# Strassen's block products in half of the contraction of a down projection's unit pairs, one pipeline for all pairs, and the mixer's tables loaded in the mixer

## What is computed

```python
def swiglu(h, w1, w3, w2):
    return (jax.nn.silu(h @ w1) * (h @ w3)) @ w2

h = rmsnorm(x, g_ffn1[l])
x = x + 0.5 * swiglu(h, w1_a[l], w3_a[l], w2_a[l])
h = rmsnorm(x, g_mix[l])
...                       # in-projection, two attentions, gates, out-projection
h = rmsnorm(x, g_ffn2[l])
x = x + 0.5 * swiglu(h, w1_b[l], w3_b[l], w2_b[l])
return rmsnorm(x, g_final)
```

## Time and profile before

| | |
|---|---|
| time, median of 3 runs | 1125.85 us (1125.63 to 1126.07) |
| the profiled execution's own time | 1127.22 us |
| its span | 1125.3 us |
| mean granted TensorE clock | 0.997 of full speed |
| PE busy, matmuls | 1101.4 us (98%), 6033 |
| DVE busy | 770.2 us (68%), 1090 |
| ACT busy | 543.7 us (48%), 870 |
| share of the 16 DMA engines, main queue | 28.9% |

### The profile page before, as it was taken

How to read it: one execution, slowest core, us unless ns; L and a number is a source line. 1 busy time by engine, 2 the same in 40 slices (tenths; PEclk the granted TensorE clock), 3 DMA queues, 4 the chain that set the end, 5 groups by cost and what they waited for, 6 DMA issues and landing times.

```text
span 1125.3 us, 15594 instructions
## 1 busy us (share of the span) xinstructions
PE 1101.4 (98%) x6033; PEld 943.5 (84%) x6033; DVE 770.2 (68%) x1090; ACT 543.7 (48%) x870; POOL 2.7 (0%) x6
## 2 busy tenths in 40 slices
PE   8999999999999999999999999999999999999996
PEld 6888899988998788877777778788898899889985
DVE  7876378745868778678765556667774578637864
ACT  6554155523644456567755543425552355415642
POOL 0000000000000000000000000000000000000000
PEclk9999999999999999999999999999999999999999
DMA  8323233332324212111112113422233323333222
GB/s 295 96 75 113 75 113 113 113 94 94 93 73 131 79 39 75 56 38 53 51 57 75 52 57 96 142 94 94 90 104 106 95 94 113 94 94 113 82 68 75
DMA packets 34295, 103.18 MB, mean 92 GB/s; under 512 B 4144, under 2 KB 7472, under 8 KB 34224
## 3 DMA queue, kind: packets, MB, share of 16 engines
q1 hardware_dynamic: 34224, 102.21, 28.9%
HBM read 100.10 MB, written 2.10 MB: 91 GB/s over the span
## 4 chain that ended last, share of the span: by engine, by line
PE 85%; DVE 6%; ACT 4%; issue 3%; SPq 1%; DMA 1%; POOL 0%; POOLq 0%; DVEq 0%; ACTq 0%
PE acc_pair L1208 24%; PE acc_pair L1209 24%; PE acc_pair L1210 24%; PE pair_bank L1208 2%; PE pair_bank L1210 2%; PE pair_bank L1209 2%; DVE w_lo L785 1%; PE bank L1208 1%; PE bank L1210 1%; PE bank L1209 1%; ACT rope L646 1%; ACT w_hi L487 1%; DMA w_raw<-in_w13a 1%; PE bank L1216 1%; PE bank L1218 1%
## 5 line engine op out<-in xcount | busy, mean ns | idle before, releaser
L1208 PE MATMUL acc_pair<-xg_hi,w_hi 128*128 128x512 f32 (+1 forms) x693 | 265.5, 383 | 1.5 <-DVE w_lo L1016 1.5
L1209 PE MATMUL acc_pair<-xg_lo,w_hi 128*128 128x512 f32 (+1 forms) x693 | 259.8, 375 | 0.0
L1210 PE MATMUL acc_pair<-xg_hi,w_lo 128*128 128x512 f32 (+1 forms) x693 | 259.1, 374 | 0.0
L487 ACT ACTIVATE w_hi<-w_raw 128x1024 fp32r<-128x1024 f32 (+3 forms) x159 | 154.3, 976 | 147.9 <-PE acc_pair L1210 147.3
L785 DVE TENSOR_TENSOR w_lo<-w_raw,w_hi 128x1024 fp32r<-128x1024 f32 (+3 forms) x159 | 178.6, 1126 | 42.3 <-ACT w_hi L487 41.3
L1210 PEld LDWEIGHTS acc_pair<-xg_hi,w_lo 128*128 128x128 f32 x693 | 130.5, 188 | 24.6
L1208 PEld LDWEIGHTS acc_pair<-xg_hi,w_hi 128*128 128x128 f32 x693 | 130.8, 189 | 23.1 <-issue 2.8
L1209 PEld LDWEIGHTS acc_pair<-xg_lo,w_hi 128*128 128x128 f32 x693 | 131.0, 189 | 19.9 <-issue 0.7
L1210 PE MATMUL acc_pair<-hid_hi,w_lo 128*128 128x512 f32 x352 | 138.8, 394 | 0.0
L1209 PE MATMUL acc_pair<-hid_lo,w_hi 128*128 128x512 f32 x352 | 138.2, 393 | 0.0
L1208 PE MATMUL acc_pair<-hid_hi,w_hi 128*128 128x512 f32 x352 | 136.9, 389 | 0.0
(11 more groups left out here) (220 smaller groups left out, 2059.7 us busy)
## 6 DMA issues: line engine op xcount, KB each, us to landing
w_raw<-in_w13b SPq DMA_DIRECT2D x44, 512.0 KB, 3.6
w_raw<-in_w13a SPq DMA_DIRECT2D x40, 512.0 KB, 3.8
w_raw<-in_wmix SPq DMA_DIRECT2D x22, 512.0 KB, 3.5
w_raw<-in_w2a SPq DMA_DIRECT2D x16, 512.0 KB, 3.6
w_raw<-in_w2b SPq DMA_DIRECT2D x16, 512.0 KB, 3.5
w_raw<-in_wgate SPq DMA_DIRECT2D x8, 512.0 KB, 3.5
w_raw<-in_wend SPq DMA_DIRECT2D x8, 512.0 KB, 3.5
w_raw<-in_wo SPq DMA_DIRECT2D x8, 512.0 KB, 3.5
```

The costliest lines, as they stand in the source:

```text
L487: act.activation(w_hi[:, s, 0:width], w_raw[:, s, 0:width], ACT.Copy).then_inc(whi_done, 1)
L1208: pe.matmul(o, w_h, r_h, start=first, stop=False, skip_group_check=check)
L1209: pe.matmul(o, w_h, r_l, start=False, stop=False, skip_group_check=check)
L1210: return pe.matmul(o, w_l, r_h, start=False, stop=last, skip_group_check=check)
```

## The change

The down units are run in pairs as well: of the 8 tiles (6 in the last chunk) of contraction, 4 are multiplied as 7 block products of 2 tiles and 256 columns (`HQ = 2`), the others as before. This is done for all down pairs but the last of each FFN, so for 11 pairs in each. The hidden tiles' sums are made by DVE while the gate and up pairs run: whenever the second tile of a block pair of `hid_pairs` has been multiplied, `hidden_sums` makes four sums of 256 columns (into the two `sq` buffers, as `hsum`), ACT splits off `th_hi`, DVE `th_lo`. The order of the down weights' tiles follows (`hid_order`). Gate, up and down pairs go through one `fast_pair` on each engine, in which the work on the pair before (`take_pair` or `take_outputs`) comes at fixed places. `cos`, `sin`, `mask_dl`, `rope2` and `roped` move to the mixer's room; the three loads are issued in the mixer and DVE's multiplication of the tables stands ahead of its part in the first scores.

```diff
+HQ = 2
+HID_PAIRS = {(0, 0): ((0, 1), (4, 5)), (1, 0): ((2, 3), (4, 5))}
...
+def hid_pairs(b, c):
+    return HID_PAIRS.get((b, c), ((0, 1), (2, 3)))
...
+def hid_order(b, c):
+    pairs = hid_pairs(b, c)
+    front = [p[0] for p in pairs] + [p[1] for p in pairs]
+    return front + [k for k in range(CHUNKS[c][1]) if k not in front]
...
+def fast_pairs(b):
+    base = (FFN_A, FFN_B)[b]
+    units = []
+    for c, (f0, n) in enumerate(CHUNKS):
+        at = chunk_base(base, c)
+        units += [at + 2 * j for j in range(n) if f0 + j >= PLAIN[b]]
+        units += [at + 2 * n + m for m in range(0, KD - (2 if c == len(CHUNKS) - 1 else 0), 2)]
+    return units
...
+def hidden_pair(u):
+    b, c, j = gate_tile(u)
+    for q, p in enumerate(hid_pairs(b, c)):
+        if p[1] == j:
+            return HQ * (len(CHUNKS) * b + c) + q
+    return None
...
...
                 load(u, 0, A["wmix"][u - MIX])
+                if u == MIX + 5:
+                    sp.wait_ge(unit_done, MIX)
+                    sp.dma_start(cos[:], A["cos"]).then_inc(late_loaded, 16)
+                    sp.dma_start(sin[:], A["sin"]).then_inc(late_loaded, 16)
+                    sp.dma_start(mask_dl[:].bitcast(mybir.dt.uint16), A["mask_dl"]).then_inc(late_loaded, 16)
...
+            def hidden_sums_hi(u):
+                h = hidden_pair(u)
+                if h is not None:
+                    act.wait_ge(hsum_done, 4 * (h + 1))
+                    act.activation(th_hi[:, :, h % HQ, :], hsum, ACT.Copy).then_inc(th_hi_done, 1)
...
+            def squares(u, n_next):
+                _, _, m = down_unit(u)
+                for k in (0, 1):
+                    act.wait_ge(acc_read[(u + k) % RING], reads(u + k, 0) + 1)
+                    square(m + k, n_next)
+            def fast_pair(u, prev, nxt, n_next):
                 g = fast_index(u)
                 r1, r3, r4, r2 = quarters(u)
+                before = gate_tile(prev) if prev is not None else None
+                turn = before is not None and down_unit(u) is not None
+                f = hidden_tile(prev)
                 split_hi(u + 2, 0, unit_width(u + 2))
                 act.wait_ge(p6_done, g + 1)
                 act.activation(r3, r2, ACT.Copy, scale=-1.0).then_inc(seed2, 1)
@@ -574,43 +668,43 @@
                     act.wait_ge(p5_added, g)
                 act.activation(p5[:, 0], bank_p5, ACT.Copy, scale=-1.0).then_inc(p5_copied, 1)
                 act.activation(p5[:, 1], bank_p5, ACT.Copy).then_inc(p5_copied, 1)
+                if turn:
+                    silu(prev, f)
                 act.wait_ge(p7_done, g + 1)
                 act.activation(r4, r2, ACT.Copy).then_inc(seed3, 1)
-                if not first:
-                    silu(u - 2, f - 1)
-                if last:
+                if turn:
+                    hidden_hi(f, before[2])
+                elif before is not None:
+                    silu(prev, f)
+                if prev is not None and before is None and down_unit(prev)[1] == len(CHUNKS) - 1:
+                    if down_unit(prev)[2] == 0:
+                        act.preload_act_table_set("sqrt_and_others")
+                    squares(prev, n_next)
+                if nxt is None:
                     split_hi(u + 3, 0, unit_width(u + 3))
                 else:
                     split_second_hi(u + 3)
-                if not first:
-                    hidden_hi(f - 1, slot - 1)
-                if last:
-                    silu(u, f)
-                    hidden_hi(f, slot)
-                else:
-                    seed_first(u + 2)
...
+            def ffn(b, n_norm, n_next):
+                plain_pairs((FFN_A, FFN_B)[b], NF * b, n_norm)
+                pairs = fast_pairs(b)
+                for u, prev, nxt in zip(pairs, [None] + pairs, pairs[1:] + [None]):
+                    fast_pair(u, prev, nxt, n_next)
+                u = pairs[-1] + 2
+                for k in (0, 1):
+                    if u + k + 2 < UNITS:
+                        split_hi(u + k + 2, 0, unit_width(u + k + 2))
+                    if k == 0:
+                        squares(u - 2, n_next)
+                    act.wait_ge(acc_read[(u + k) % RING], reads(u + k, 0) + 1)
+                    square(KD - 2 + k, n_next)
...
+            def add_fifth(u):
+                g = fast_index(u)
+                dve.wait_ge(unit_done, u + 2)
+                dve.wait_ge(p5_copied, 2 * (g + 1))
+                late = acc_pair[u % RING // 2][:].rearrange("p (n c) -> p n c", n=2)[:, :, HALF:SEQ]
+                dve.tensor_tensor(late, late, p5, ALU.add).then_inc(p5_added, 1)
+                dve.wait_ge(p5_added, g + 1)
...
+            def hidden_sums(u):
+                h = hidden_pair(u)
+                if h is None:
+                    return
+                f = hidden_tile(u)
+                b11, b12 = prod[:, (f - 1) % 2, 0:HALF], prod[:, (f - 1) % 2, HALF:SEQ]
+                b21, b22 = prod[:, f % 2, 0:HALF], prod[:, f % 2, HALF:SEQ]
+                dve.wait_ge(prod_done, f + 1)
+                if h:
+                    dve.wait_ge(th_hi_done, h)
+                    dve.wait_ge(th_lo_done, h)
+                dve.tensor_tensor(hsum[:, 0], b12, b11, ALU.subtract).then_inc(hsum_done, 1)
+                dve.tensor_tensor(hsum[:, 2], b12, b22, ALU.subtract).then_inc(hsum_done, 1)
+                dve.wait_ge(hsum_done, 4 * h + 1)
+                dve.tensor_tensor(hsum[:, 1], b22, hsum[:, 0], ALU.subtract).then_inc(hsum_done, 1)
+                dve.wait_ge(hsum_done, 4 * h + 3)
+                dve.tensor_tensor(hsum[:, 3], b21, hsum[:, 1], ALU.subtract).then_inc(hsum_done, 1)
+            def hidden_sums_lo(u):
+                h = hidden_pair(u)
+                if h is not None:
+                    dve.wait_ge(hsum_done, 4 * (h + 1))
+                    dve.wait_ge(th_hi_done, h + 1)
+                    dve.tensor_tensor(th_lo[:, :, h % HQ, :], hsum, th_hi[:, :, h % HQ, :].bitcast(F32),
...
+            def take_outputs(u, n_next):
+                _, c, m = down_unit(u)
+                add_fifth(u)
+                for k in (0, 1):
+                    s, before = update_x(u + k, m + k, 0.5)
+                    if c == len(CHUNKS) - 1:
+                        if n_next < 3:
+                            dve.wait_ge(acc_read[s], before + 1)
+                            prep(m + k, n_next)
+                        add_square(m + k, n_next)
+            def fast_pair(u, prev, nxt, n_next):
+                before = gate_tile(prev) if prev is not None else None
+                turn = before is not None and down_unit(u) is not None
+                f = hidden_tile(prev)
+                if before is not None:
+                    take_pair(prev, f)
+                elif prev is not None:
+                    take_outputs(prev, n_next)
+                split_lo(u + 2, 0, unit_width(u + 2))
+                if turn:
+                    multiply(prev, f)
+                if nxt is not None:
+                    weight_sums(nxt)
+                if turn:
+                    hidden_lo(f, before[2])
+                elif before is not None:
+                    multiply(prev, f)
+                    hidden_sums(prev)
+                if nxt is not None:
+                    split_second_lo(u + 3)
+                    split_sums_lo(nxt)
+                else:
+                    split_lo(u + 3, 0, unit_width(u + 3))
+                if before is not None and not turn:
+                    hidden_lo(f, before[2])
+                    hidden_sums_lo(prev)
...
             for kind, w in MIX_STEPS:
+                if kind == "scores" and w == 0:
+                    dve.wait_ge(late_loaded, 16 * N_LATE)
+                    for table in (cos, sin):
+                        strided = table[:].rearrange("c (r p) -> c r p", r=DIL)
+                        dve.tensor_tensor(strided, strided, rstd[:].rearrange("c (p r) -> c r p", r=DIL),
+                                          ALU.mult).then_inc(tables_done, 1)
                 if kind in ("Ua", "Us"):
                     split_lo(w + 2, 0, unit_width(w + 2))
                 elif kind == "norm":
                     norm(w)
                     take_out(MIX)
-                    for table in (cos, sin):
-                        strided = table[:].rearrange("c (r p) -> c r p", r=DIL)
-                        dve.tensor_tensor(strided, strided, rstd[:].rearrange("c (p r) -> c r p", r=DIL),
-                                          ALU.mult).then_inc(tables_done, 1)
...
+            def rest_of_unit(u, last):
                 s = u % RING
-                for k in range(2 * Q, KD):
+                if down_unit(u) is None:
+                    places = [] if last else [(k, xg(k)) for k in range(2 * Q, KD)]
+                else:
+                    b, c, m = down_unit(u)
+                    order = hid_order(b, c)
+                    places = []
+                    for k in range(2 * HQ, len(order)):
```

(36 more changed lines are left out.)

308 lines of the change are left out of this document (150 added, 158 removed).

## The result

The changed kernel takes 1143.14 us, median of 6 runs (1142.44 to 1144.24), beside 1125.96 us for the kernel before (6 runs, 1125.63 to 1129.93): a ratio of 1.0146, 95% interval 1.0131 to 1.0161. It is 17.2 us slower. The direction was forecast (+7.8), the size was not, and the time lies above the range. The profiled execution has a span of 1141.5 us (own time 1143.33), 16.2 more than before, and a mean granted clock of 0.986 instead of 0.997.

The account below looks back on a forecast made before the run. PE was taken as the bound (85% of the chain, 98% busy). Terms -10.4 + 6.8 + 7.5 + 4.3 + 0.3 - 0.7 = +7.8 us on the median 1125.85 gave 1133.7 us, range 1128.5 to 1139.8.

Parts of the forecast that it names:

- the clock: PE's granted clock behind stands in the FFNs: no term in the sum, a fall considered only as rival C.
- rival C: Four FFN stands of 3.2 or 3.5 us each bring near 1.5 us at 1.2 GHz: 1139.7 us, chance 0.15.
- Start and tail: Start: five loads instead of eight, PE not waiting for them, 0; outputs' backlog after the first FFN delaying the norm, +0.2 us.
- Part 1: Down pairs on PE: block products shorten 16 pairs by 0.47 us and 6 by 0.48, -10.4 us.
- Part 2: Third block of down pairs: PE waits for ACT's late seed, 16 x 0.37 and 6 x 0.15, +6.8 us.
- Part 3: Last chunks: DVE's squares ahead of the next weights' split, and a late tile at the turn, hold PE, +7.5 us.
- Part 4: Plain pairs: hidden-tile sums delay the splits and PE, 2.07 us in the second FFN, 2.27 in the first, +4.3 us.
- Part 5: Fast gate and up pairs: hidden-tile sums on DVE hold PE by some 0.1 us now and then, +0.3 us.
- Part 6: Mixer and tail: table products leave DVE's chain before the first scores, -0.9; with the norm's delay -0.7 us.

Follow-up runs that it names:

- Experiment 5: Changed kernel with ACT splitting the next pair's weights between the two seeds in every output pair, fifth product's copies last: 1138.34 us, ratio 1.0086.
- experiment 2: Changed kernel with ACT's seeds ahead of the weight split in the first two chunks' output pairs, DVE's multiply before its split at the turn: 1140.34 us, ratio 1.0103.
- experiment 1: Changed kernel with DVE's next-norm preparation and sums of squares moved behind the next weights' splits in the last chunk: 1131.62 us, ratio 1.0032.
- experiment 3: Changed kernel with the splits of the plain pairs' hidden-tile sums moved to the first fast pair: 1132.27 us, ratio 1.0038.
- experiment 6: Kernel before with ACT's split repeated once ahead of the seed in the second FFN's first fast pair: 1130.59 us, ratio 1.0027.
- experiment 10: Kernel before with ACT's split repeated three times ahead of the seed in the second FFN's first fast pair: 1132.13 us, ratio 1.0046.
- 7: Kernel before with ACT's split repeated twice ahead of the seed in the second FFN's first fast pair: 1131.67 us, ratio 1.0031.

## Why the prediction was wrong

Its sum of products and stands was right to 3 us; the step that failed is the one that left the clock out of the sum, rival C at a chance of 0.15 where it should have been the forecast. The 7.3 us behind the four stands carry 1133.7 to 1141. Start and tail add 3.6 more, and what was mis-sized in parts 1, 2 and 5 takes 2.7 off.

- **Part 1, forecast -10.4:** the pair of 10.44 instead of 10.99 makes 0.55, and over all pairs the two FFNs show -6.0 and -5.8, -11.8. It was mis-sized by 1.4: in a block product a 256-column matmul takes 0.113 to 0.119, and part 1 took 0.119 for all. The Trainium skill's gap ("TensorE: Matmul & The Clock Gate", section "Back-to-back issue gap") would have given 13; the measured gain is between the two.
- **Part 2, +6.8:** 16 x 0.31 = 5.0 in the first chunks, 0.6 and 0.3 in the last ones, so about 5.8. Place, releaser and count are right, 0.37 was 0.06 too much. Experiment 5 takes them away, experiment 2 moves them.
- **Part 3, +7.5:** 3.31 + 3.32, 0.50, 2 x 0.24 = 7.6. Right to 0.1, and undone by experiment 1. What it didn't say is that the order buys something as well: the operands of the mixer's first unit.
- **Part 4, +4.3:** the second FFN 2.02 (2.07 forecast), undone by experiment 3. In the first FFN, from the start of DVE's reciprocal to the end of PE's wait it is 60.61 - 26.09 = 34.52 us before and 64.82 - 28.02 = 36.80 after: 2.28, forecast 2.27.
- **Part 5, +0.3:** 0; no stand beside fast pairs.
- **Part 6, -0.7:** the stand before the mixer's first scores (0.87) is gone. Mixers without a low clock take 395.97 to 396.06 us in the copies of the kernel before and 395.24 to 395.26 in those of the changed one: -0.75, forecast -0.9. The low clock of the earlier trace rows went with that stand, and 1.6 with it (397.60 us before), but another came at 522 and costs as much (396.90), so leaving it out was right by luck.
- **The clock, forecast 0:** +1.59, +1.66, +2.62, +1.47. C's mechanism and its four places were right; its price, four times 1.5, was a little low.
- **Start and tail, forecast 0 and +0.2:** at the start 2.9 us of matmul time at a low clock (7.5 to 13.2) delay the norm by 0.8 and DVE's reciprocal by 1.9, and the 1.9 arrive on PE. In the tail the last 16 matmuls of 128 columns took 3.78 us instead of 2.05, and the tail is 1.7 longer.

Start and tail don't belong to the change. The last matmuls' line is, in the changed kernel, in the profile of the kernel before, and in experiment 6:

```profile
1130.59 3.78 PE L1654 MATMUL pair_bank<-identf,col 128*128 128x128 f32 x16 [0.70 <-DVE col L1345]
```

```profile
1116.03 2.05 PE L1486 MATMUL pair_bank<-identf,col 128*128 128x128 f32 x16 [0.70 <-DVE col L1198]
```

```profile
1115.42 3.61 PE L1490 MATMUL pair_bank<-identf,col 128*128 128x128 f32 x16 [0.70 <-DVE col L1202]
```

Nothing of the tail is edited in experiment 6, and it takes 3.61 too (3.48 and 3.07 in experiments 10 and 7): the 2.05 of the first profile is the only one under 3 in all thirteen. A low clock at the start is in six of the nine profiles with the change, and in one (experiment 10) of the four without. It comes with a first matmul of weights at 7.4 to 7.7 us, but also with one at 6.6 to 7.0, and one at 7.37 (experiment 6) is without it, so the first load's landing alone doesn't decide it. Whether the change makes it likelier stays open.

In sum: the forecast +7.8, with -1.4 for part 1, +7.3 for the clock in the FFNs, +1.9 and +1.7 for start and tail, -1.0 for part 2 and -0.3 for part 5 is +16.0, beside a difference of 16.2 between the profiles; 0.2 I can't place. (The medians differ by 17.2, since the profiled execution of the kernel before was 1.3 above its median.)

What went wrong in the thinking: against C I wrote that behind the stand of 1.31 no low clock shows. A short stand that is harmless says nothing on one two and a half times as long. And the Trainium skill's rule (same page, section "Why this matters for your kernels": keep PE from standing idle between bursts, or it drops back to half clock) spoke for C. The measurements agree with it in most cases, 19 of 21 stands of 3.3 us and more, not in all.

## What to carry to other kernels

Where PE is the bound, price a stand twice: by its length, and, where it is as long as these (2.2 us and more), by 1.4 to 2.7 us that can be lost at half clock behind it, which no list of waits shows. Block products that cut PE's blocks from 9 matmuls to 6 also shorten the cover of everything that is handed over between them; here they gained 11.8 us and lost 17.7 in stands, and 7.3 at a low clock behind them, until the order on ACT and DVE was made anew, and only then did the change pay (0.6%). And ask where in a pair an operand is wanted first: moving a split by 2.8 us "to the end" only moved the wait to the middle of the pair.

## What the runs showed of the hardware

Stands of PE in the FFNs, at the norm ahead of the first and ahead of the mixer's first unit, and the loss at a low clock behind them, from the nine profiles with the change and the four without it:

| stand, us | count | followed by a low clock | loss, us |
|---|---|---|---|
| 3.3 to 4.7 | 21 | 19 | 1.5 to 2.7 |
| 2.1 to 2.7 | 12 | 4 | 1.4 to 1.6 |
| 0.9 to 1.9 | some 30 | 0 | 0 |

The two exceptions above are 3.31 and 3.26 us long and are the same stand as one that lost 1.66, begun 1.6 and 5.5 us earlier in the span. Other places say the same: ahead of the mixer's first unit 2.52 us, begun at 371.3, had a fall behind it, and 2.54 and 2.58, begun at 368.4 and 364.0, had none; the stand of 3.49 us lost 2.6 us begun at 816.7, and 1.6 begun at 813.7. The length alone thus doesn't decide it. What these cases differ in is when the stand begins, so shifting a kernel by a few us can add or remove a stretch. That is read from kernels that differ elsewhere too; no run moved a stand and nothing else. In the mixer, whose matmuls are shorter and use 64 rows in part, shorter stands seem to do it too: all thirteen profiles have a stand of 1.56 us near 500. Of the nine with the change, three have a fall 1.9 to 2.1 us behind its end, which makes the mixer 0.8 us longer, three have one 13 us later, next to a stand of 0.64, at a cost of 1.6 us, and three have none; one of 1.6 came behind the stand of 0.86 in two of the four without it. Two kernels that differ elsewhere can differ by 1.6 us there for no reason of their own.
